# The high part of the first piece of x: made by VectorE instead of ScalarE

## The reference

```
def rms_norm(x, g):
    xf = x.astype(jnp.float32)
    y = xf * lax.rsqrt(jnp.mean(xf * xf, axis=-1, keepdims=True) + RMS_EPS)
    return (y * g.astype(jnp.float32)).astype(x.dtype)

h = rms_norm(x, pre_mix_g[l])
# hybrid_mixer: columns of h @ w_in -> q, k, v of every branch, and three gates
(q_n, k_c, v_c, k_s, v_s, k_w, v_w, g_n, q_m, k_m, v_m, q_x,
 gate_nsa, gate_moba, gate_mem) = split_columns(h @ w_in)
```

## Time and profile before

| | |
|---|---|
| median of 3 runs | 424.48 us (424.45 to 424.70) |
| profiled execution | 424.4 us, span 422.6 us |
| PE busy | 409.8 us, 97% of the span |
| DVE busy | 269.9 us, 64% |
| ACT busy | 242.8 us, 57% |
| POOL busy | 44.4 us, 11% |
| moved by DMA | 78.82 MB, mean 187 GB/s |

### The profile page before, as it was taken

How to read it: one execution, slowest core, us unless ns; L and a number is a source line. 1 busy time by engine, 2 the same in 40 slices (tenths; PEclk the granted TensorE clock), 3 DMA queues, 4 the chain that set the end, 5 groups by cost and what they waited for, 6 DMA issues and landing times.

```text
span 422.6 us, 5888 instructions
## 1 busy us (share of the span) xinstructions
PE 409.8 (97%) x2054; PEld 331.9 (79%) x2054; DVE 269.9 (64%) x472; ACT 242.8 (57%) x417; POOL 44.4 (11%) x78
## 2 busy tenths in 40 slices
PE   8999989999999999999999999999999999999994
PEld 4777778887787788778787788888888888888883
DVE  4854996985676587639957765655565555445434
ACT  6654976578767766743557584455445544545321
POOL 6210030022121212217000000000000000000000
PEclk9999999999999999999999999999999999999999
DMA  8999993634435333448355557666555656665002
GB/s 297 392 331 375 371 299 111 199 101 126 174 106 173 121 101 113 173 139 324 106 193 175 174 168 236 194 185 208 167 172 174 190 197 199 199 193 187 19 2 99
DMA packets 52016, 78.82 MB, mean 187 GB/s; under 512 B 2076, under 2 KB 28488, under 8 KB 51992
## 3 DMA queue, kind: packets, MB, share of 16 engines
q1 hardware_dynamic: 50216, 73.52, 53.1%
q0 software_dynamic: 1344, 4.43, 3.2%
q10 hardware_dynamic: 432, 0.56, 0.4%
HBM read 77.43 MB, written 1.07 MB: 186 GB/s over the span
## 4 chain that ended last, share of the span: by engine, by line
PE 86%; DVE 6%; ACT 3%; issue 3%; DMA 1%; DVEq 0%; ACTq 0%
PE acc L1162 24%; PE acc L1164 24%; PE acc L1163 24%; PE ob L1398 3%; PE ptb L1366 2%; PE sbank L1311 1%; PE ptb L1477 1%; PE sbank L1312 1%; PE acc L1201 1%; PE acc L1205 1%; ACT wh L479 1%; PE acc L1206 1%; DMA gx<-in_gx 1%; PE sbank L1273 1%; DVE wl L772 1%
## 5 line engine op out<-in xcount | busy, mean ns | idle before, releaser
L772 DVE TENSOR_TENSOR wl<-raw,wh 128x1024 fp32r<-128x1024 f32 (+1 forms) x126 | 152.6, 1218 | 89.2 <-ACT wh L479 88.6
L479 ACT ACTIVATE wh<-raw 128x1024 fp32r<-128x1024 f32 (+1 forms) x126 | 130.7, 1045 | 89.6 <-PE acc L1164 78.6
L1162 PE MATMUL acc<-wh,xh 128*128 128x512 f32 (+1 forms) x368 | 144.3, 392 | 1.1 <-DVE xl L807 1.1
L1164 PE MATMUL acc<-wh,xl 128*128 128x512 f32 (+1 forms) x368 | 142.1, 386 | 0.0
L1163 PE MATMUL acc<-wl,xh 128*128 128x512 f32 (+1 forms) x368 | 141.9, 386 | 0.0
L1162 PEld LDWEIGHTS acc<-wh,xh 128*128 128x128 f32 x368 | 69.1, 188 | 14.6 <-issue 1.5
L1164 PEld LDWEIGHTS acc<-wh,xl 128*128 128x128 f32 x368 | 69.1, 188 | 14.2
L1163 PEld LDWEIGHTS acc<-wl,xh 128*128 128x128 f32 x368 | 69.2, 188 | 12.3
L1162 PE MATMUL acc<-wh,ah 128*128 128x512 f32 x88 | 34.3, 390 | 0.0
L1164 PE MATMUL acc<-wh,al 128*128 128x512 f32 x88 | 34.3, 389 | 0.0
L1163 PE MATMUL acc<-wl,ah 128*128 128x512 f32 x88 | 34.2, 389 | 0.0
(11 more groups left out here) (198 smaller groups left out, 447.7 us busy)
## 6 DMA issues: line engine op xcount, KB each, us to landing
raw<-in_w_in SPq DMA_DIRECT2D x18, 1024.0 KB
raw<-in_w_ffn_gate SPq DMA_DIRECT2D x22, 512.0 KB
raw<-in_w_ffn_up SPq DMA_DIRECT2D x22, 512.0 KB
raw<-in_w_ffn_down SPq DMA_DIRECT2D x22, 512.0 KB
raw<-in_w_mix_out SPq DMA_DIRECT2D x4, 1024.0 KB
raw<-in_w_mem_kv SPq DMA_DIRECT2D x2, 1024.0 KB
raw<-in_w_nsa_o SPq DMA_DIRECT2D x2, 1024.0 KB
raw<-in_w_in SPq DMA_DIRECT2D x3, 512.0 KB, 7.3
```

The source lines that it names most:

```text
L479: nc.scalar.activation(wh[:, k, :, 0:w], raw[:, slot, 2 * half:2 * half + 2, 0:w], ACT.Copy).then_inc(hi_done, 1)
L772: nc.vector.tensor_tensor(wl[:, k, :, 0:w], raw[:, slot, 2 * half:2 * half + 2, 0:w], wh[:, k, :, 0:w].bitcast(F32), ALU.subtract).then_in ...
L1162: nc.tensor.matmul(bank[:, 0:w], h[:, k, c], wh[:, slot, s, 0:w], start=first, stop=False)
L1164: return nc.tensor.matmul(bank[:, 0:w], l[:, k, c], wh[:, slot, s, 0:w], start=False, stop=last)
```

## The change

The high part of piece 0 of x is made by DVE, as its first step after the memset of eps, with TENSOR_SCALAR (multiplication by the gain, output in fp32r). ACT starts with the weights of piece 0 instead and makes the high parts of pieces 1 to 7 as before. A new semaphore, xh0_done, tells x_lo(0) on DVE and the first product on TensorE that the high part is there. Since ACT's counter xh_done now starts with piece 1, x_lo(k) waits for one less. TensorE had no wait of its own for xh: ACT made it before wh, and hi_done covered both.

```
+        xh0_done = sem("xh0_done")
...
-            for k in range(PIECES):
+            first_hi(0)
+            for k in range(1, PIECES):
                 x_hi(k)
                 first_hi(k)
...
             def x_lo(k):
-                dve.wait_ge(xh_done, k + 1)
+                if k == 0:
+                    dve.wait_ge(xh0_done, 1)
+                else:
+                    dve.wait_ge(xh_done, k)
...
+            dve.wait_ge(xtd[0], 16)
+            nc.vector.tensor_scalar(xh[:, 0], xt0[:, 0], gcol[:, KD:KD + 1], None, ALU.mult).then_inc(xh0_done, 1)
             for k in range(PIECES):
                 x_lo(k)
                 first_lo(k)
...
                 for k in range(PIECES):
                     slot, s = k // 2, k % 2
+                    if k == 0:
+                        pe.wait_ge(xh0_done, 1)
                     pe.wait_ge(hi_done, k + 1)
```

## The result

| | median us | executions |
|---|---|---|
| before | 424.47 (424.21 to 426.27) | 20 |
| changed | 425.30 (424.66 to 425.65) | 20 |

The ratio is 1.0015, with a 95% interval of 1.0009 to 1.0022: the changed kernel is slower by 0.4 to 0.9 us. (The medians differ by 0.83 us, the means by 0.66.) The median of 425.30 is the upper end of the forecast range of 424.1 to 425.3 to the digit, and inside the 0.2% that were called no change. But 20 executions tell it from none. The profiled execution took 425.15 us (span 423.4), 0.75 us more than that of before.

The account below looks back on a forecast made before the run. After the first gx transfer, TensorE's stream of products bounds the kernel (busy 97%). The early lead cancels to 0; 424.4 us plus 0.1 for a remainder of the held case gives 424.5, range 424.1 to 425.3.

Parts of the forecast that it names:

- nothing is gained: At the start: TensorE's earlier start is lost at piece 2, which waits for its transfer; sum -0.24 + 0.24 = 0.
- the lead: First product on TensorE at 5.18 instead of 5.42, 0.24 us earlier, with the lead zero at 9.39.
- The hold: At the start: DVE's new step held to the end of klo's memset at 6.22, ending at 6.52.
- rival (c): Held, and DVE's late chain moves requests and landings: 1.2 us reach the end, 425.6, or 1.8 us, 426.2; chance 0.07.
- TensorE is 1.2 us late: If DVE's step is held, TensorE's low products of piece 2 start at 10.6 instead of 9.39.
- the sign I gave for the held case: If held, the gap before 32.72 shrinks from 0.97 to near nothing, the product after it within 0.25 us of 32.72.
- The slack: TensorE's 0.97 us wait before 32.72 absorbs its lateness of 1.2 us, leaving 0.23 us at most.
- (b): DVE's step held, lateness hidden in the gap at 32.72: 424.4 to 424.65; the forecast case, chance 0.48.
- my argument against (c): Transfers don't wait for TensorE; the request at 10.27 moves by some 0.8 us at most while the queue is full.

Follow-up runs that it names:

- e1: Changed kernel with GpSimd's memset of klo starting only after DVE has made the high part of x piece 0: 424.52 us.
- e2: Changed kernel with the DVE step written as a two-input TENSOR_TENSOR instead of TENSOR_SCALAR, memset beside it as before: 424.58 us.
- e12: Repeat of e10, the changed kernel with klo's memset ahead of GpSimd's four small transfers: 425.01 us.
- e10: Changed kernel with GpSimd's memset of klo moved ahead of its four small transfers: 425.80 us.
- e4: Changed kernel with two more warm-up products of 512 columns on TensorE during the wait for DVE: 424.50 us.
- e9: Changed kernel with a second GpSimd memset of 3072 columns just ahead of klo's: 428.16 us.
- e3: Changed kernel with GpSimd's memset of klo cut into 12 of 256 columns each: 424.58 us.
- e6: Changed kernel with GpSimd's two copies of bias values held back until DVE's fourth eviction is done: 425.31 us.
- e7: Kernel before, with TensorE's first product also waiting for GpSimd's four large memsets, ACT and DVE as before: 424.40 us.
- e5: Changed kernel run again without an edit: 425.47 us, 1.0017 of the kernel before.
- e11: Kernel before, with GpSimd's memset of klo moved ahead of its four small transfers and nothing else: 425.99 us.

## Why the prediction was right or wrong

- **That nothing is gained: right.** ACT's first rounding is 0.6 us earlier, its pieces 1 and 2 still wait for their transfers (piece 2 starts at 7.73, I had 7.49). e1 and e2 show the lead itself: first product 0.40 us earlier (I had 0.24, from a modelled end of the warm-up products), time unchanged.
- **The hold: right in kind, too short.** I let it end with klo's memset, at 6.22; the small memsets behind it counted too, and the step ended at 6.93 instead of 6.52. I had named this only inside rival (c), as 1.8 us late. e1 and e2 show that GpSimd's memset is the cause and the one-input form the condition. Free of a memset, the step takes 0.35 to 0.49 us (e1, e12, e10), where I took 0.3 and had 0.48 as the dear end.
- **The step that failed: "TensorE is 1.2 us late".** It was 2.63 us late at the bias product. The hold's part was 1.55 (e4), and 1.1 us came from the clock, which I had read as full all through because the profile of before gives 1.00 in every window. The column still gives 1.00 for the changed kernel, so it could not have told me; the distance of the products could. The sum had no term for the clock at which the products after an idle stretch run. It is probably also what makes the executions differ by 0.8 us, since e4, with TensorE kept busy, lies within 0.36; that isn't shown. And the sign I gave for the held case, the transposes within 0.25 us of 32.72, failed: they came at 34.23.
- **The slack: too small.** I had the gap of 0.97 us at 32.72 and left 0.23 at most. It swallows 1.1 us (2.63 to 1.51), 0.46 more are gone by 48.24 and up to 0.58 by 58.15, together 2.17 to 2.19 (e9, e3, e6). The two errors nearly cancelled: 1.4 us too little lateness against 1.2 us too little slack. That the time stayed in the range at all, at its very end and 0.8 us above the forecast of 424.5, is luck, not insight.
- **Why 0.75 was left.** 2.63 - 2.19 = 0.44 us is lateness beyond the slack. The other 0.3 us is a loss that no step had: the late chain lets GpSimd's copies start first at 54.96, and DVE's steps beside them take 0.29 us longer (0.08 + 0.21); e6 takes it away and finds 0.23, in single traces.
- **Rival (c)** (held, and the landings move) can be ruled out: the landing of 39.64 is at 39.70, and the rounding of 29.63 starts at 29.04. The end was on the slower side by another road, (b) with a larger lateness than its slack. But my argument against (c) was incomplete. I wrote that the transfers don't wait for TensorE and looked at the request of 10.27 alone, which moved by 0.8 us (11.07) as I said. The request of 15.79 waits for the bias product, and moved by 2.63 us (to 18.42), the one of 18.14 behind it by 2.56. The landings held all the same; how late a request may come before they move no run shows.
- **My own theory T**, that TensorE's lateness alone is what costs, fell with e7.

## What to carry to other kernels

Before a step goes to DVE, look at what GpSimd does in that moment: here a one-input DVE step of 0.35 us took 2.58 us beside a long memset, and the same product in a two-input form took 0.42 us. Where TensorE waits at the start of a kernel, count the wait once and then ask what clock the products after it get. Read that clock from the distance of the products too: the column of the granted clock gave 1.00 in a stretch where 8 products took 3.50 us. A slack is the sum over all later places where the engine waits for transfers, not the first gap alone; and a step whose successors wait for transfers, as ACT's here, isn't worth moving.

## What the runs showed of the hardware

- A DVE TENSOR_SCALAR from SBUF to SBUF (128x256) that starts during a GpSimd memset is held to its end, and through further ones that follow without a gap: 2.58 us for one large and four small ones, 5.25 us for two large and four small ones, 1.61 us with twelve of 0.27 us each, where DVE got in behind the ninth, the sixth from its start. A TENSOR_TENSOR of the same size isn't held (0.42 us), and the TENSOR_SCALAR beside GpSimd's requests of transfers isn't either (0.49 and 0.42 us; 0.35 in e1).
- The other way round, a GpSimd copy that starts first stretches DVE's two-input subtractions: from 2.35 to 2.56 us for two, while the copies take 0.84 instead of 2.79 us.
- Around an idle stretch TensorE's clock was at the lower level for some time, with products of 512 columns 0.43 us apart instead of 0.23. With a granted clock of 0.50: from 7.2 to 10.6 us in e5 (idle for 2.23 us before), from 7.6 to 10.9 in e3 (1.15 us), from 35.2 to 38.4 in e11 (2.73 us), from 34.4 to 37.7 in e12 (2.11 us). In the first profile of the changed kernel (1.42 us idle) the products were as far apart until 10.75, with a granted clock of 1.00 in the column. In e7 1.56 us of idle time had no such stretch behind it in the profiled execution, and none of its 12 executions was long. What tells the cases apart these runs don't show.
